# A hybrid decoder layer on one core: w_out's pieces through four buffers instead of two, and a gap in the plan ahead of the second half

## The reference, cut to what matters

```
h   = x + concat(sparse attention, retention) @ w_out      # w_out: 1024 x 1024
xn  = rms_norm(h) * norm_ffn_w
q   = xn @ w_q                                             # 8 heads x 2 halves x 64
s1, s2 = q . sub_keys_1, q . sub_keys_2                    # 128 scores per half
v1, i1 = top16(s1); v2, i2 = top16(s2)
eid = ids of the top16 of v1[i] + v2[j]                    # per head: 16 experts
y   = sum over the 128 chosen experts of softmax * gelu(u_emb[eid] . xn) * v_emb[eid]
out = rms_norm(h + y) * final_norm_w
```

## Time and profile before

| what | value |
|---|---|
| median of three runs | 3763.69 us |
| the profiled execution's own time | 3768.69 us |
| its span, first to last instruction | 3766.9 us |
| TensorE matmul busy | 3155.9 us (84%) |
| VectorE busy | 2595.1 us (69%) |
| ScalarE, GpSimd busy | 1251.1, 1237.9 us (33% each) |
| moved by the DMA engines | 1242.28 MB, 330 GB/s over the span |
| gathers of rows (line 1834) | 1056, 1128.34 MB with the sample tile's, on the queue of GpSimd |
| pieces of w_out | 72, 512 KB each, 7.7 us from issue to landing (median) |

### The profile page before, as it was taken

The page is one execution under the profiler, slowest core; times in us unless marked ns, Lnnn a source line. Parts: engine busy times, 40 slices in busy tenths (PEclk is TensorE's granted clock), DMA queues, the critical chain, the costliest instruction groups (busy, mean ns, idle before and its releaser), DMA issues.

```text
span 3766.9 us, 31960 instructions
## 1 busy us (share of the span) xinstructions
PE 3155.9 (84%) x9551; PEld 1545.3 (41%) x9551; DVE 2595.1 (69%) x6052; ACT 1251.1 (33%) x3568; POOL 1237.9 (33%) x1084
## 2 busy tenths in 40 slices
PE   9999766988798879878987899689887389896876
PEld 4444443543354335434543454245433244342421
DVE  1222248778868878888888888898846988443645
ACT  1111122453245326422642264226233033321322
POOL 0000002444344434433443344334342034442433
PEclk9999877999999999989999999899988689997999
DMA  5111126999999999999999999899998179997998
GB/s 202 54 49 47 63 75 261 417 421 422 369 409 421 410 367 409 413 377 387 417 419 355 375 391 420 327 378 405 366 393 330 54 304 421 421 387 269 421 421 342
DMA packets 190142, 1242.28 MB, mean 330 GB/s; under 512 B 22672, under 2 KB 27152, under 8 KB 50640
## 3 DMA queue, kind: packets, MB, share of 16 engines
q0 software_dynamic: 155520, 1128.34, 73.6%
q1 hardware_dynamic: 34448, 111.89, 7.9%
HBM read 1218.76 MB, written 20.72 MB: 329 GB/s over the span
## 4 chain that ended last, share of the span: by engine, by line
PE 46%; DMA 26%; DVE 21%; ACT 3%; issue 3%; POOL 1%; SPq 0%; ACTq 0%; DVEq 0%; POOLq 0%
PE yacc L1029 24%; DMA weights<-in_uv,eid 20%; PE bank L854 11%; DVE weights L1485 6%; DVE kv L1348 4%; DVE tiny L1347 3%; PE bank L992 3%; PE bank L966 2%; DMA weights<-in_w_out 2%; PE bank L918 1%; PE bank L942 1%; DVE weights L1214 1%; DMA kv<-in_cache_ik,gi 1%; DMA out_y_p<-nw 1%; POOL weights L1834 1%
## 5 line engine op out<-in xcount | busy, mean ns | idle before, releaser
L1029 PE MATMUL yacc<-weights,diag 128*128 128x512 f32 (+1 forms) x4224 | 1970.2, 616 | 233.2 <-ACT diag L1754 233.0
L1834 POOL DMA_INDIRECT weights<-in_uv,eid x1056 | 1210.3, 1146 | 2469.1 <-PE yacc L1029 1802.1
L1485 DVE CUSTOM_DVE_ANT_0 weights<-weights,xn 128x1024 f32<-128x1024 f32 x1056 | 1274.3, 1224 | 602.3 <-DMA weights<-in_uv,eid 589.1
L1029 PEld LDWEIGHTS yacc<-weights,diag 128*128 128x128 f32 (+1 forms) x4224 | 795.0, 194 | 1298.0 <-issue 910.1
L1744 ACT ACTIVATE gl<-hv 128x2 f32<-128x2 f32 x528 | 107.1, 203 | 1512.6 <-DVE hv L1485 1511.4
L1754 ACT ACTIVATE diag<-main,coef 128x128 f32<-128x128 f32 x1024 | 359.3, 394 | 161.6 <-PE yacc L1029 145.7
L1747 ACT ACTIVATE coef<-gl,gate 128x1 f32<-128x1 f32 x1056 | 253.3, 287 | 17.3
L966 PE MATMUL bank<-weights 128*128 128x512 f32 (+1 forms) x288 | 157.9, 685 | 108.4 <-DMA weights<-in_w_out 106.5
L1347 DVE MAX8 tiny<-kv 128x8 f32<-128x384 f32 (+6 forms) x224 | 245.0, 1094 | 3.1
L1348 DVE MATCH_REPLACE8 kv<-tiny,kv 128x384 f32<-128x384 f32 (+6 forms) x224 | 241.6, 1079 | 0.0
L854 PE MATMUL bank<-weights 128*128 128x512 f32 (+1 forms) x560 | 230.8, 574 | 3.0 <-DMA weights<-in_w_in 3.0
(11 more groups left out here) (244 smaller groups left out, 2368.5 us busy)
## 6 DMA issues: line engine op xcount, KB each, us to landing
weights<-in_w_out SPq DMA_DIRECT2D x72, 512.0 KB, 7.7
weights<-in_uv,eid POOLq DMA_INDIRECT x1056, 11.5
weights<-in_w_in SPq DMA_DIRECT2D x6, 2048.0 KB, 19.5
Hb<-h_scratch SPq DMA_DIRECT2D x7, 1700.0 KB, 10.6
h_scratch<-Hb SPq DMA_DIRECT2D x4, 1700.0 KB, 5.5
h_scratch<-spare SPq DMA_DIRECT2D x3, 1700.0 KB, 5.5
nw<-in_wffn SPq DMA_DIRECT2D x9, 512.0 KB, 4.8
nw<-in_wfin SPq DMA_DIRECT2D x9, 512.0 KB, 14.0
```

Of the source, the lines that this page charges most:

```text
L1029: mm = nc.tensor.matmul(yacc[0:W, 512 * j:512 * (j + 1)], diag[:, n % 4, 0:W], ring[:, n % RING, D + 512 * j:D + 512 * (j + 1)], start=Fal ...
L1485: ins = V.tensor_tensor_reduce(u, u, xn[:, t % 2, :], 1.0, 0.0, ALU.mult, ALU.add, hv[:, n % RING:n % RING + 1])
L1834: pool.indirect_dma_start(dst, None, table, bass.IndirectOffsetOnAxis(ap=ids, axis=0)).then_inc(s, 16)
```

## The change

Four buffers take the place of two. The two new ones lie in the first 2048 columns of `keys_sb`. Piece i goes to buffer i % 4, so pieces 0, 1, 4 and 5 of a tile use the old buffers and pieces 2, 3, 6 and 7 the new ones. Pieces 0 to 3 of the first tile are asked for at the start. Later on, steps `out` 0 to 5 ask for the piece four ahead: 0 to 3 for pieces 4 to 7 of the same tile, 4 and 5 for pieces 0 and 1 of the next one. Steps `out` 6 and 7 ask for nothing. Pieces 2 and 3 of the next tile are asked for at `pick` part 7 of SyncE's list, behind a wait for `chosen` of the tile. In the planner's list the lag of the first `add` of a tile is 4.0 in place of 0.3.

```diff
@@ back_steps
         if j % 4 == 3:
-            steps.append(Step("add", t, j // 4, "D", 0.8, 1, 0.3))
+            steps.append(Step("add", t, j // 4, "D", 0.8, 1, 4.0 if j == 3 else 0.3))
@@ build
-        wout_sb = [weights[:, 8192 + 1024 * i:8192 + 1024 * (i + 1)] for i in range(2)]
+        wout_sb = [weights[:, c:c + 1024] for c in (8192, 9216, 12288, 13312)]
-        wout_in = [sem("wout_in0"), sem("wout_in1")]
+        wout_in = [sem(f"wout_in{i}") for i in range(4)]
@@ sync
             def load_wout(i):
-                sp.dma_start(wout_sb[i % 2], w_out[i % CHUNKS]).then_inc(wout_in[i % 2], 16)
+                sp.dma_start(wout_sb[i % 4], w_out[i % CHUNKS]).then_inc(wout_in[i % 4], 16)
@@ sync, load of the first tile
-                        load_wout(0)
-                        load_wout(1)
+                        for i in range(4):
+                            load_wout(i)
@@ sync, the steps
                 elif what == "out":
                     i = CHUNKS * t + part
-                    if i + 2 < CHUNKS * (TILES + 1):
-                        if part % 4 == 3:
-                            filled(sp, ("out", t, part // 4))
+                    if part < 6 and i + 4 < CHUNKS * (TILES + 1):
+                        if part == 3:
+                            filled(sp, ("out", t, 0))
                         else:
                             sp.wait_ge(out_used, 6 * t + 3 * (part // 4) + part % 4 + 1)
-                        load_wout(i + 2)
+                        load_wout(i + 4)
+                elif what == "pick" and part == 7 and t < TILES:
+                    sp.wait_ge(chosen, t + 1)
+                    load_wout(CHUNKS * (t + 1) + 2)
+                    load_wout(CHUNKS * (t + 1) + 3)
@@ tensor, out
-                pe.wait_ge(wout_in[i % 2], 16 * (i // 2 + 1))
+                pe.wait_ge(wout_in[i % 4], 16 * (i // 4 + 1))
...
-                    mm = nc.tensor.matmul(b[0:R, :], mixT[:, k, 0:R], wout_sb[i % 2][:, 512 * (k - k2):512 * (k - k2 + 1)],
+                    mm = nc.tensor.matmul(b[0:R, :], mixT[:, k, 0:R], wout_sb[i % 4][:, 512 * (k - k2):512 * (k - k2 + 1)],
```

## The result

The changed kernel took 3700.76 us (median of 4 runs, 3698.55 to 3710.33) against 3764.24 us for the kernel before in the same set. The ratio is 0.9838, interval 0.9818 to 0.9858: 61 us less, where 3705 us had been forecast. A later set gave 3701.77 us and 0.983 (0.9817 to 0.9844). The profiled execution shown here took 3710.33 us, the slowest of its four; its span is 3708.5 us.

What follows compares the result with a forecast made beforehand. DMA was taken as the limit once rows are gathered, losing time where it idles at each `out`. Terms 7.8 + 0 + 37.4 + 0 + 14 + 0 = 59.2 us off the median of 3763.69 gave about 3705 us, range 3688 to 3742.

Steps and rivals of the forecast that it cites:

- Tile 0: Before any gather, DMA idle: early pieces remove TensorE's gaps and part of its slow clock, 7.8 us (5.6 to 8.9).
- Tile 1: DMA is full from the first rows on, so only the order of bytes changes: 0 us, ends -2.5 and +2.5.
- Tile 7: No wait for w_out stands there and DMA's share is 1.00 over its pieces: 0 us gained.
- Tiles 2 to 6: At each `out`, idle DMA time of 44.9 us in all is mostly removed: 37.4 us gained (20 to 44.9).
- Piece 4 as the next wait: In tile 2, piece 4 lands at 19.6 us, needed at 21.2 us after `out` begins; 0 to 2 us wait left.
- Rival B: Wait moves to piece 4, as pieces asked for at once land one after another: 34 us less, 3730 us; 23%.
- Tile 8: TensorE bound, DMA idles 18.0 us around the eight pieces; four pieces at hand gain 14 us (8 to 18).
- SyncE's new wait: At `pick` 7 SyncE waits for `chosen`, so the final norm's weights are issued later, still 54 us ahead: cost 0.
- the gap: The longer lag in the plan lets other TensorE steps go ahead of `out` 4: 0 us, ends -5 and +5.
- C: Slower: the sample tile's top-k block from 2904 us grows, DMA idling up to 70 us more, 3775 us; 8%.
- Rival D: Boundary gains turn into idle time later, leaving tile 0's 7.8 us alone or less: 3755 to 3768 us; 7%.
- The two rules: HBM-to-SBUF binds at about 358 GB/s per core, which the trace contradicts; DMA engines take turns between queue rows with work.

Runs made afterwards that it cites:

- a3: The changed kernel, but pieces 2 and 3 of all nine tiles asked for only when pieces 0 and 1 have been used: 3741.48 us, ratio 0.9935.
- a4: The kernel before, two buffers, with SyncE's wait for the store and the norm weights moved behind `out` part 6: 3751.34 us, ratio 0.9966.
- c1: The changed kernel once more, unaltered, as anchor of a later set: 3701.77 us, ratio 0.983.
- b2: The changed kernel, but pieces 2 and 3 of tile 0 alone asked for as before the change: 3710.49 us, ratio 0.9849.
- b3: The changed kernel, but pieces 2 and 3 of tiles 2 to 6 asked for as before the change: 3730.38 us, ratio 0.9906.
- a1: The kernel before, two buffers, with only the lag of a tile's first `add` raised from 0.3 to 4.0: 3761.63 us, ratio 0.9995.
- b1: The changed kernel, but pieces 2 and 3 of tile 8 alone asked for as before the change: 3709.63 us, ratio 0.9845.
- a2: The changed kernel with the lag of a tile's first `add` back at 0.3: 3700.01 us, ratio 0.9824.
- c3: The changed kernel with SyncE's store wait and norm weights moved behind `out` part 5, and the lag back at 0.3: 3692.92 us, ratio 0.9808.

## Why the prediction was right

**Bound and mechanism.** That DMA is the limit, that time is lost where it idles, and that the wait at piece 2 makes it idle: right, shown by a3 (the wait at piece 2 back, 40 us back) and by the idle time of DMA, which falls with the time. The steps below were less right.

**Why piece 2 is late.** "Piece 2 is late because of SyncE and not because of bandwidth": this step failed for the larger part. a4 took SyncE's wait away and gained 12 of 63 us; the piece then takes 12.5 us to land in tile 2, where it took 5.8 us. Asked for at that moment, with the store, x and the gathers on the way, it is late in either order. The forecast survived since the change avoids both causes: it asks 53 to 79 us ahead in tiles 2 to 6.

**Tile 0.** Forecast 7.8 us (5.6 to 8.9). From `out` 0 to the first gather it is 124.8 us before, 119.2 changed and 117.3 in c1, so 5.6 to 7.4 us. b2 gives 7.2 us for the early pieces alone. The first gather itself came 4.7 us sooner (604.2 and 599.5), not 7 to 8, as `out` 0 began 0.9 us later. The share of the slow clock was about right: the eight pieces took 19.1 us of TensorE's time before and 18.6 now.

**Tile 1.** Forecast 0; from `out` 1 to `out` 2 it is 3.5 us longer. The two pieces of tile 2 are now loaded in this stretch, 2.5 us of bytes at 419 GB/s; every later tile passes on as much as it gets, and the last one gets 2.5 us back. Where the pieces of tile 2 come late, the stretch is shorter: 361.0 us in b3 and 358.5 in a3, 362.4 and 363.0 in the two profiles of the changed kernel. This is near the play between profiles, but it points the same way.

**Tile 7.** Forecast 0; 4.2 us longer in these two profiles, 1.2 us in c1 and 1.6 us shorter in a3, so nothing that is clear of noise.

**Tiles 2 to 6.** Forecast 37.4 us (20 to 44.9). From `out` 2 to `out` 7 the table gives 1849.8 before and 1807.5 changed, 42.3 us. Taken with a1 and c1 as well, it is 32 to 50 us. b3 keeps 11 of the 42 us with late pieces (1838.9) and a3 18, which is the depth's part; the sum had not told the two apart. It had also not named the later waits in tiles 4 to 6, 12.4 us of the 106.5. The forecast left 1.5 us of idle DMA per tile, 7.5 us in all; 2.7 us are left.

**Piece 4 as the next wait.** Forecast to land 19.6 us after the start of `out` and to be needed at 21.2. Both sizes were off. It is the first of three asked for from 971.08 us on, and they took 11.0, 14.3 and 17.3 us to land. So piece 4 was there 22.0 us after the start (971.08 + 11.0 - 960.09). TensorE came to it at 992.02 us, 31.9 us after the start: five sums stand ahead of it in tile 2, and the forecast had priced four. They wait 4.2 us in all for ScalarE's diagonal matrices, and the last takes 6.63 us in place of 3.6. With 8.0 us for a landing I took a piece asked for alone; in a row they take longer. Rival B was close to the mark in its premise and wrong in its price.

**Tile 8.** Forecast 14 us (8 to 18); 19.1 us by the table, 15.3 by c1, and 2.5 of it are the bytes above, so 13 to 17. The early pieces are 5.6 to 8.9 of that (b1). The rest goes with the wait of 6.39 us at piece 6 of the kernel before, which the prediction did not name and the depth removes. TensorE, tile 8, changed:

```profile
3378.11 7.05 PE L970 MATMUL bank<-weights 128*32 128x512 f32 x16
3385.09 7.13 PE L1033 MATMUL yacc<-weights,diag 128*128 128x512 f32 x16
3392.16 7.05 PE L970 MATMUL bank<-weights 128*32 128x512 f32 x16
```

The eight pieces and the sums run without a gap, and at the fast clock, granted 1.00 from 3378.1 to 3399.2 us. In the kernel before, after TensorE had sat idle for 6.81 us, it was 0.56 from 3427.8 to 3434.1 us, near the lower of the two levels (1.2 and 2.4 GHz). Eight matmuls took 6.31 us there, 0.79 each; here sixteen take 7.05 us, 0.44 each.

**SyncE's new wait, the gap, rivals C and D.** The pieces went out at 880.82 us and the final norm's weights behind them at 881.67, 79 us ahead of `out`, and the store that needs the latter went out 2.8 us after the start of `out` as before: cost 0, as said. The gap: 0 (a1, a2, c3). The block of top-k rounds of the sample tile has not grown:

```profile
2856.00:2936.00 80.00, 0.00 (x0) 0.00 (x0) 78.28 (x66) 0.35 (x1) 0.00 (x0) 0.52 0.17 72
```

VectorE works 78.28 of 80 us and DMA idles there as before; it is now by far the largest hole. DMA moves nothing for 82.5 us before (2914.0 to 2996.5 us) and for 80.0 us here (2870.5 to 2950.5), while C needed a block 59 us longer. Rival D's price (tile 0's gain alone) is ruled out by the result, and b3 shows the part of tiles 2 to 6.

**The sum.** The total agrees better than its terms, and that is in part luck. In the two profiles the terms of tiles 2 to 6 and of tile 8 were 10 us too small together, and tiles 1 and 7, put at 0, were 7.7 us longer.

**The two rules.** The kernel moved 384 to 411 GB/s through the stretches of tiles 2 to 6 above, so it is not held at 358 GB/s. But the prediction left out the condition of that figure: the Trainium skill, DMA: Bandwidth & Descriptors, Bandwidth, gives about 358 GB/s per core for the case that both cores of a pair stream, and 425 GB/s as measured for one core alone. One core runs here, and its 419 GB/s agree with the latter. That the engines take turns between queue rows (the Trainium skill, same page, Queues, rings and completion order) fits in its direction: a piece behind two transfers of its own queue, beside full gathers, took 12.5 us, where one alone took 8.0. The prediction said that the 8.0 us fit the rule, but the size does not. A piece on idle engines took 3.2 us (asked for at 1691.42 us in the kernel before); half of the bandwidth would add 1.25 us for its bytes, an estimate of 4.5 us, and 8.0 was measured. What makes up the rest is open. No run here has both cores of a pair at work.

## What to carry to other kernels

Where a queue is the limit, count its idle time around a wait, not the wait: 106.5 us of waiting were worth 63 us, and a3 gained 22 us with the wait at piece 2 in full length, as other bytes filled part of the hole and later waits went. Load what the next stage needs first at a time when nothing waits for it, into a buffer that is idle then; asking 6 to 9 us sooner in a full queue brought it only 1.2 to 4.0 us sooner. Two remedies for one hole do not add, and bytes moved past a boundary can show up as a loss on the other side of it. And look at every wait in the line of a total, not only at the longest: 18.8 of the 106.5 us stood at later pieces of tiles 4 to 6 and 8.

## What was not expected of the hardware

A piece of 512 KB came 5.8 us after it was asked for at 972.91 us in the kernel before (978.75 - 972.91), when the gathers were running dry, 8.0 us alone beside full gathers, and 12.5 us when asked for 0.5 us behind x and 0.9 us behind the store (a4). On idle engines it took 3.2 us. All these pieces have the same size, so its landing is set by what is on the way with it.
